# Expert loop of a hybrid network: gather with the tokens as the loaded side, and biases spread over four row groups of 32

## The chip, the core and the metric

The kernel runs on one core of one Trainium2 chip. A core has TensorE (PE, whose weight loads the profile lists apart as PEld), VectorE (DVE), ScalarE (ACT), GpSimd (POOL), SyncE (SP) and 16 DMA engines. The metric is the device time of one execution, in microseconds.

## What is computed

Two blocks run one after the other on 256 tokens of 1024 features in f32. The change lies in the last stage of the second block, a mixture of experts: 32 experts, four chosen for each token, each a clamped SwiGLU layer with two biases. The core of the reference:

```python
xb = h[tok_b]                                  # tokens of expert e
u = xb @ w1[e] + b1[e]                         # 1024 -> 2048
glu = jnp.minimum(u[:, 0::2], SWIGLU_LIMIT)
lin = jnp.clip(u[:, 1::2], -SWIGLU_LIMIT, SWIGLU_LIMIT)
act = glu * jax.nn.sigmoid(SWIGLU_ALPHA * glu) * (lin + 1.0)
return act @ w2[e] + b2[e]                     # 1024 -> 1024
...
out = out.at[slot_tok].add(slot_gate * y)      # weighted sum over the experts
```

## The kernel before

Everything is written by hand for each engine: one instruction stream per engine, ordered as the code stands, with semaphores between them. The first 1,660 us are the hybrid layers and the mixer, which the change leaves alone. Then `moe_tensor`, `moe_scalar`, `moe_vector`, `moe_pool` and `moe_loads` (SP) run the experts.

**Ahead of the loop.** The router's gates (`gate_map`, tokens x experts) are turned to `gT` (experts x tokens) by L2529 and a ScalarE copy; h is turned to `h_tok` (tokens on partitions, L2513 and the copy L2673). `start_sums` (L2539) opens the output sums in banks 0 to 3 with b2 times gT, 32 rows each. L2549 gathers for the first turn.

**The loop** runs once per job: 32 experts and as many more as there are experts with over 64 tokens; here 33 turns. One job takes at most 64 tokens (`SLOTS`). A turn `t` on PE, in order:

- L2592, the first bias: `bsel` (one-hot of the expert, 32 rows x 64 columns) is loaded and b1 (32 rows) streams, 512 columns at a time, into banks 4 and 5, halves 0 and 1 (`side`) on 64 output partitions each.
- L2601, the first product: `hsel` (gathered rows, turned) is loaded, four weight units of 2 MiB stream from the ring. After each unit e_unit is raised, and SP may overwrite the slot.
- L2549, `gather()` for turn t+1: `sel` (tokens x 64 slots, from VectorE) is loaded, `h_tok` streams, into bank 6 on 2 x 64 partitions.
- L2563, `scatter()`: the output of turn t-1 (`ye`) times `selgT` is added to banks 0 to 3.
- L2614 turns `selg` (the gates) into bank 7, ScalarE copies it to `selgT` (L2708).
- L2555, `turn_gathered()`: ScalarE has copied bank 6 to `gsel` (L2685); four transposes put it back into bank 6 turned, ScalarE copies that to `hsel` (L2688), which the next L2601 loads.
- L2621 turns `hid` (VectorE's activation) into bank 7 once `selgT` is copied; ScalarE copies it to `hidT` (L2712).
- L2629, the second product: two weight units. Then ScalarE copies to `ye` (L2715).

**The transfers.** SP issues the six units of turn t+1 one by one as the slots come free (L2438 for the first four, L2440 for the last two), after waiting for `e_unit`. There are six slots; at turn 16 the last two units come from `extra`, which is loaded ahead. b1 and b2 are loaded by L2450 after `grids`; PE and VectorE wait for all three (`late_in`).

Of the kernel before, what the change touches and what calls it, by code (L numbers as in the profile page):

```python
# [2324 lines left out]
EXTRA = 16  # L2325
JOBS = N_EXPERTS + EXTRA
# [19 lines left out]
def moe_grids():  # L2346

    o, e = np.meshgrid(np.arange(EXTRA), np.arange(N_EXPERTS), indexing="ij")
    grids = np.broadcast_to(np.concatenate([o.reshape(-1), e.reshape(-1)]), (P, 2 * GRID))
    return np.concatenate([grids, np.arange(P)[:, None]], axis=1).astype(np.float32)  # L2350


def moe_signals(ctx, nc, g, hyb):
# [22 lines left out]
def moe_memory(ctx, nc, g):  # L2376
# [8 lines left out]
    sb("b2", [D], parts=N_EXPERTS)  # L2385
    sb("b1", [2 * D_FF], parts=N_EXPERTS)
# [19 lines left out]
    sb("gT", [T], parts=N_EXPERTS)  # L2406
# [3 lines left out]
    sb("selgT", [T])  # L2410
    sb("gsel", [4 * P])
# [6 lines left out]
    sb("ye", [4 * P])  # L2418
# [13 lines left out]
def moe_loads(sp, nc, g):  # L2432
# [16 lines left out]
    for dst, what in (("grids", g["grids_dram"]), ("b2", g["b2_dram"][0]), ("b1", g["b1_dram"][0])):  # L2449
        sp.dma_start(g[dst][:, :], what).then_inc(g["late_in"].sem, g["late_in"].one())  # L2450
# [36 lines left out]
MOE_LOOP = ("e_unit", "u_first", "ga_done", "st_done", "gb_done", "ht_done")  # L2487


def moe_tensor(pe, nc, g):  # L2490
# [41 lines left out]
    def start_sums(first):  # L2532

        if first == 0:
            pe.wait_ge(g["turned_out"].sem, g["turned_out"].at(None, 2))
            pe.wait_ge(g["gates_out"].sem, g["gates_out"].at(None, 1))
            pe.wait_ge(g["late_in"].sem, g["late_in"].at(None, 3))
# [30 lines left out]
    pe.wait_ge(g["sel_ready"].sem, g["sel_ready"].at(None, 0))  # L2568
    gather().then_inc(g["ga_done"].sem, 1)
# [8 lines left out]
    def job(t, kept=0):  # L2578
# [37 lines left out]
        pe.wait_ge(g["ga_out"].sem, g["ga_out"].at(t, 1))  # L2616
        turn_gathered().then_inc(g["gb_done"].sem, g["gb_done"].one())
# [41 lines left out]
def moe_scalar(act, nc, g):  # L2659
# [408 lines left out]
```

## Time and profile before

| | us |
|---|---|
| median of 3 runs | 2665.75 |
| lowest, highest | 2664.05, 2666.48 |
| the profiled execution | 2661.23 |
| its span, first to last instruction | 2658.4 |
| PE busy | 2544.8 |
| VectorE busy | 924.9 |
| ScalarE busy | 583.4 |

The profiled execution is 4.5 us shorter than the median, and 2.8 us of it lie outside the span. All stretches below are in microseconds from the start of the span. A plain f32 matmul of the program is two load records and two matmul records in the trace, a transpose is one of each.

### The profile page before, as it was taken

How to read it: one execution, taken by the hardware profiler on the slowest of the kernel's cores; microseconds unless marked ns; L12 is line 12 of the kernel's file. 1: busy time of each engine (PE TensorE's matmuls, PEld its weight loads, DVE VectorE, ACT ScalarE, POOL GpSimd, SP SyncE). 2: the span in 40 equal slices, each digit the busy share in tenths (PEclk: the TensorE clock that was granted, in tenths of full speed). 3: DMA queues.
4: the chain of work that ended last, by engine and by line, in shares of the span. 5: the costliest groups of instructions: out<-in, count | busy, mean ns of one | idle time of the engine just before them, and what ended most of it. 6: DMA issues, size and time to landing. Idle time of an engine off the chain costs nothing.

```text
span 2658.4 us, 42182 instructions
## 1 busy us (share of the span) xinstructions
PE 2544.8 (96%) x18014; PEld 1673.4 (63%) x18014; DVE 924.9 (35%) x2004; ACT 583.4 (22%) x1168; POOL 149.5 (6%) x124
## 2 busy tenths in 40 slices
PE   8999999999999999999997889899999999999998
PEld 6867878888884887888886777433333333333333
DVE  1863363312277245323476653311111111111112
ACT  2100233301100123220135433311111111111112
POOL 0050000000032000000003220000000000000000
PEclk9999999999999999999999999999999999999999
DMA  7555232344455422336410002999999999999995
GB/s 262 198 182 198 100 122 98 124 158 159 175 204 176 173 95 96 127 128 214 162 64 4 4 4 108 420 428 428 428 428 429 428 428 427 429 428 428 429 427 251
DMA packets 135029, 636.13 MB, mean 239 GB/s; under 512 B 5120, under 2 KB 5392, under 8 KB 109136
## 3 DMA queue, kind: packets, MB, share of 16 engines
q1 hardware_dynamic: 133904, 629.78, 59.6%
q0 software_dynamic: 992, 4.37, 0.5%
q8 instruction: 109, 1.79, 0.3%
q14 instruction: 24, 0.20, 0.0%
HBM read 633.08 MB, written 1.05 MB: 239 GB/s over the span
## 4 chain that ended last, share of the span: by engine, by line
PE 94%; ACT 2%; DVE 2%; issue 1%; DMA 1%; SPq 0%; ACTq 0%; DVEq 0%
PE bank L268 26%; PE bank L2601 17%; PE bank L2629 9%; PE bank L459 6%; PE bank L1405 4%; PE bank L481 4%; PE bank L289 4%; PE bank L1356 4%; PE bank L2563 2%; PE bank L2592 2%; PE bank L2549 2%; PE bank L1664 1%; PE bank L357 1%; PE bank L2621 1%; ACT hidT L2712 1%
## 5 line engine op out<-in xcount | busy, mean ns | idle before, releaser
L268 PE MATMUL bank<-hT,ring 128*128 128x256 f32 x3136 | 689.8, 380 | 2.5 <-DMA ring<-in_w_in 1.4
L268 PEld LDWEIGHTS bank<-hT,ring 128*128 128x128 f32 x3136 | 592.8, 190 | 94.6 <-issue 13.3
L2601 PE MATMUL bank<-ring,hsel 128*64 128x512 f32 x2112 | 462.0, 595 | 0.0
L2601 PEld LDWEIGHTS bank<-ring,hsel 128*64 128x64 f32 x2112 | 149.0, 137 | 310.8 <-issue 310.5
L2874 DVE TENSOR_SCALAR glu<-bank 128x256 f32<-128x256 f32 x66 | 28.0, 425 | 754.2 <-PE bank L2601 750.9
L2629 PE MATMUL bank<-ring,hidT 128*64 128x512 f32 x1024 | 226.8, 595 | 22.0 <-ACT hidT L2712 22.0
L754 DVE SCALAR_TENSOR_TENSOR a_buf<-v_pad,par,a_buf 128x256 f32<-128x256 f32 x480 | 215.8, 529 | 0.0
L2629 PEld LDWEIGHTS bank<-ring,hidT 128*64 128x64 f32 x1024 | 70.5, 137 | 156.2 <-issue 128.1
L1405 PE MATMUL bank<-ring 64*64 64x64 f32 (+1 forms) x5696 | 133.3, 229 | 25.6 <-issue 9.3
L1405 PEld LDWEIGHTS bank<-ring 64*64 64x64 f32 x5696 | 120.9, 137 | 40.6 <-issue 12.1
L2703 ACT ACTIVATE sig<-glu 128x256 f32<-128x256 f32 x66 | 27.5, 417 | 458.8 <-DVE glu L2874 458.8
L289 PE MATMUL bank<-ring,hT 128*128 128x512 f32 x256 | 111.4, 594 | 0.0
L481 PE MATMUL bank<-ro,ring 128*128 128x256 f32 x512 | 111.4, 379 | 0.0
L481 PEld LDWEIGHTS bank<-ro,ring 128*128 128x128 f32 x512 | 97.0, 190 | 13.8 <-issue 0.8
L1356 PE MATMUL bank<-stack,ring 128*128 128x256 f32 x480 | 104.5, 379 | 0.0
L1356 PEld LDWEIGHTS bank<-stack,ring 128*128 128x128 f32 x480 | 91.1, 190 | 12.7 <-issue 0.3
L289 PEld LDWEIGHTS bank<-ring,hT 128*128 128x128 f32 x256 | 48.2, 190 | 60.0 <-issue 60.0
L1232 POOL TENSOR_TENSOR ring<-ring,mcons 128x256 f32<-128x256 f32 x80 | 62.4, 815 | 250.9 <-DVE ring L2173 250.9
L2715 ACT ACTIVATE ye<-bank 128x512 f32<-128x512 f32 x33 | 19.7, 597 | 237.2 <-PE bank L2629 237.2
L2563 PEld LDWEIGHTS bank<-selgT,ye 64*128 64x128 f32 x544 | 49.7, 186 | 33.0 <-issue 26.8
L2563 PE MATMUL bank<-selgT,ye 64*128 64x256 f32 x544 | 67.9, 389 | 0.8 <-ACT finrow L2717 0.8
L2549 PE MATMUL bank<-h_tok,sel 128*64 128x512 f32 x272 | 64.2, 592 | 0.5 <-DVE sel L2796 0.5
(435 smaller groups left out, 2467.6 us busy)
## 6 DMA issues: line engine op xcount, KB each, us to landing
ring<-in_w SPq DMA_DIRECT2D x196, 2048.0 KB, 16.7
ring<-in_w_in SPq DMA_DIRECT2D x66, 2048.0 KB, 7.8
ring<-in_w_ada SPq DMA_DIRECT2D x12, 2048.0 KB, 8.0
ring<-in_w_ret_out SPq DMA_DIRECT2D x8, 2048.0 KB, 7.8
ring<-in_w_out SPq DMA_DIRECT2D x6, 2048.0 KB, 8.6
ring<-in_w_conv_out SPq DMA_DIRECT2D x4, 2048.0 KB, 8.3
ring<-in_w_attn_out SPq DMA_DIRECT2D x4, 2048.0 KB, 8.0
extra<-in_w SPq DMA_DIRECT2D x2, 2048.0 KB, 34.7
```

The source lines that it names most:

```text
L268: mm = nc.tensor.matmul(out[:, j, :], w[:, k, col + j * P:col + (j + 1) * P], rhs[:, k, :], start=(k == 0), stop=(k == DC - 1))
L289: mm = nc.tensor.matmul(out[:, :, :].rearrange("p a b -> p (a b)"), g["hT"][:, k, t * P:(t + 1) * P], w[:, k, :], start=(k == 0), stop=(k ...
L459: mm = nc.tensor.matmul(out[:, j, :], ws[k // DC][:, k % DC, cols + j * P:cols + (j + 1) * P], rhs[:, k, :], start=(k == 0), stop=(k == n ...
L481: mm = nc.tensor.matmul(out[:, j, :], w[:, k, col:col + P], g["ro"][:, row * DC + k, :], start=(row == 0 and j == 0 and k == 0), stop=(row ...
L754: ins = nc.vector.scalar_tensor_tensor(out=y[:, c, :], in0=v[:, c, t:t + T], scalar=w, in1=y[:, c, :], op0=ALU.mult, op1=ALU.add)
L1232: nc.gpsimd.tensor_tensor(g["cut"][:, k, d * NC:(d + 1) * NC, :], g["MP"][:, d * NC:(d + 1) * NC, :], row(mask[:, k, d, :], NC), ALU.mult) ...
L1356: mm = nc.tensor.matmul(flat[(q + 3) % 4][:, 0:T], w[:, k, j * P:(j + 1) * P], g["stack"][:, k, lo:lo + T], start=(k == 0), stop=(k == DC ...
L1405: mm = nc.tensor.matmul(out[at:at + 64], lhsT[lo:lo + 64], rhs[lo:lo + 64], start=start, stop=stop, skip_group_check=not (start and stop))
L2549: mm = nc.tensor.matmul(half(flat[6], side), g["sel"][:, t, :], g["h_tok"][:, t, side * UNIT:(side + 1) * UNIT], start=(t == 0), stop=(t = ...
L2563: mm = nc.tensor.matmul(g["bank"][b][:, at, :], half(g["ye"], side)[:, n * P:(n + 1) * P], half(g["selgT"], side), start=False, stop=last, ...
L2601: mm = nc.tensor.matmul(half(flat[4 + b], side), g["hsel"][:, 2 * (j % 2) + k, j // 2, :], w[:, at:at + UNIT], start=False, stop=(j == 3 a ...
L2629: mm = nc.tensor.matmul(half(flat[7], side), g["hidT"][:, c, j, :], w[:, at:at + UNIT], start=(j == 0 and c == 0), stop=(j == 1 and c == 3))
```

## The change

- `gather()` swaps the sides: `h_tok` is the loaded side (128 columns with a step of 4, so that the order of the features is the one `hsel` needs), `sel` with its 64 columns streams. The result in bank 6 is already turned. It takes 16 matmuls of 64 columns instead of 4 of 512.
- `turn_gathered()`, `gsel`, `take_gathered()` and the semaphores `ga_out` and `gb_done` are gone. ScalarE copies bank 6 to `hsel` right after the gather.
- b1 and b2 are cut in four parts and loaded to four groups of 32 partitions, by eight DMAs instead of two. `bsel` and `gT` are repeated on the four groups. The four matmuls of the first bias use one group each; `start_sums` is called once and goes round the four groups, one bank each.
- The gate map is turned by eight plain matmuls into four groups of 32 output partitions instead of two transposes.
- The first gather waits for `h_tok`'s second half.

```diff
+GROUPS = P // N_EXPERTS
...
-    for dst, what in (("grids", g["grids_dram"]), ("b2", g["b2_dram"][0]), ("b1", g["b1_dram"][0])):
-        sp.dma_start(g[dst][:, :], what).then_inc(g["late_in"].sem, g["late_in"].one())
+    sp.dma_start(g["grids"][:, :], g["grids_dram"]).then_inc(g["late_in"].sem, g["late_in"].one())
+    for name, width in (("b2", D // GROUPS), ("b1", 2 * D_FF // GROUPS)):
+        for q in range(GROUPS):
+            sp.dma_start(g[name][q * N_EXPERTS:(q + 1) * N_EXPERTS, :],
+                         g[name + "_dram"][0, :, q * width:(q + 1) * width]).then_inc(g["late_in"].sem, g["late_in"].one())
...
     for t in range(TC):
-        mm = nc.tensor.transpose(flat[7][0:N_EXPERTS, t * P:(t + 1) * P], g["gate_map"][:, t, 0:N_EXPERTS], ident)
+        for q in range(GROUPS):
+            mm = nc.tensor.matmul(flat[7][q * N_EXPERTS:(q + 1) * N_EXPERTS, t * P:(t + 1) * P], g["gate_map"][:, t, 0:N_EXPERTS],
+                                  ident, start=True, stop=True)
...
-        for n in range(first, first + 4):
-            nc.tensor.matmul(g["bank"][n // 2][:, n % 2, :], g["b2"][:, n * P:(n + 1) * P], g["gT"][:, :],
-                             start=(n % 2 == 0), stop=False, skip_group_check=True)
+        for i in range(2):
+            for q in range(GROUPS):
+                lo, hi = q * N_EXPERTS, (q + 1) * N_EXPERTS
+                nc.tensor.matmul(g["bank"][q][:, i, :], g["b2"][lo:hi, i * P:(i + 1) * P], g["gT"][lo:hi, :],
+                                 start=(i == 0), stop=False, skip_group_check=True)
...
     def gather():
 
-        for t in range(TC):
-            for side in range(2):
-                mm = nc.tensor.matmul(half(flat[6], side), g["sel"][:, t, :], g["h_tok"][:, t, side * UNIT:(side + 1) * UNIT],
-                                      start=(t == 0), stop=(t == 1))
-        return mm
-
-    def turn_gathered():
         for c in range(4):
-            mm = nc.tensor.transpose(flat[6][:, c * P:(c + 1) * P], g["gsel"][:, c::4], ident)
+            for j in range(2):
+                for t in range(TC):
+                    mm = nc.tensor.matmul(flat[6][:, (2 * c + j) * SLOTS:(2 * c + j + 1) * SLOTS],
+                                          g["h_tok"][:, t, j * UNIT:(j + 1) * UNIT][:, c::4], g["sel"][:, t, :],
+                                          start=(t == 0), stop=(t == 1))
         return mm
...
     pe.wait_ge(g["sel_ready"].sem, g["sel_ready"].at(None, 0))
+    pe.wait_ge(g["turned_out"].sem, g["turned_out"].at(None, 2))
     gather().then_inc(g["ga_done"].sem, 1)
-    start_sums(0)
-    pe.wait_ge(g["ga_out"].sem, g["ga_out"].at(None, 0))
-    turn_gathered().then_inc(g["gb_done"].sem, 1)
-    start_sums(4)
+    start_sums()
...
         for b in range(2):
             for side in range(2):
-                at = (2 * side + b) * UNIT
-                nc.tensor.matmul(half(flat[4 + b], side), g["bsel"][0:N_EXPERTS, :], g["b1"][:, at:at + UNIT], start=True, stop=False)
+                lo, hi = (2 * side + b) * N_EXPERTS, (2 * side + b + 1) * N_EXPERTS
+                nc.tensor.matmul(half(flat[4 + b], side), g["bsel"][lo:hi, :], g["b1"][lo:hi, :], start=True, stop=False)
...
-        pe.wait_ge(g["ga_out"].sem, g["ga_out"].at(t, 1))
-        turn_gathered().then_inc(g["gb_done"].sem, g["gb_done"].one())
...
         act.wait_ge(g["ga_done"].sem, g["ga_done"].at(t, 1))
-        take_gathered().then_inc(g["ga_out"].sem, g["ga_out"].one())
+        take_rows().then_inc(g["gt_out"].sem, g["gt_out"].one())
         act.wait_ge(g["st_done"].sem, g["st_done"].at(t, 1))
         nc.scalar.activation(g["selgT"][:, :], flat[7][:, 0:T], ACT.Copy).then_inc(g["st_out"].sem, g["st_out"].one())
-        act.wait_ge(g["gb_done"].sem, g["gb_done"].at(t, 1))
-        take_rows().then_inc(g["gt_out"].sem, g["gt_out"].one())
```

PE in a turn of the loop, from the end of the first product to the second product. A row names output, streamed side and loaded side, and the count; h_tok is the tokens, sel the choice. Before:

```order
L2601 MATMUL bank<-ring,hsel 64x512 x8
L2549 MATMUL bank<-h_tok,sel 64x512 x4
L2563 MATMUL bank<-selgT,ye 128x256 x8
L2614 MATMUL bank<-shared_cons,selg 128x128 x2
L2555 MATMUL bank<-shared_cons,gsel 128x128 x4
L2621 MATMUL bank<-shared_cons,hid 128x128 x4
L2629 MATMUL bank<-ring,hidT 64x512 x16
```

And now:

```order
L2602 MATMUL bank<-ring,hsel 64x512 x8
L2556 MATMUL bank<-sel,h_tok 128x64 x16
L2566 MATMUL bank<-selgT,ye 128x256 x8
L2615 MATMUL bank<-shared_cons,selg 128x128 x2
L2620 MATMUL bank<-shared_cons,hid 128x128 x4
L2628 MATMUL bank<-ring,hidT 64x512 x16
```

The gather has 16 instructions of 64 streamed columns in the place of 4 of 512, and no transposes stand between those of selg and those of hid.

PE ahead of the loop, from the gates to the first product (b is b2 in L2539 and b1 in L2592). Before:

```order
L2529 MATMUL bank<-shared_cons,gate_map 32x128 x2
L2549 MATMUL bank<-h_tok,sel 64x512 x4
L2539 MATMUL bank<-gT,b 128x256 x4
L2555 MATMUL bank<-shared_cons,gsel 128x128 x4
L2539 MATMUL bank<-gT,b 128x256 x4
L2592 MATMUL bank<-b,bsel 64x512 x4
```

And now:

```order
L2533 MATMUL bank<-shared_cons,gate_map 32x128 x8
L2556 MATMUL bank<-sel,h_tok 128x64 x16
L2545 MATMUL bank<-gT,b 128x256 x8
L2593 MATMUL bank<-b,bsel 64x512 x4
```

The opening of the sums is in one piece; its count and that of the first bias are unchanged, only their rows differ.

## Rows read from the trace of the kernel before

**Rows 1.** The page: engine busy times, and the chain by engine.
```profile
PE 2544.8 (96%) x18014; PEld 1673.4 (63%) x18014; DVE 924.9 (35%) x2004; ACT 583.4 (22%) x1168; POOL 149.5 (6%) x124
...
PE 94%; ACT 2%; DVE 2%; issue 1%; DMA 1%; SPq 0%; ACTq 0%; DVEq 0%
```

**Rows 2.** The chain in order of time, one turn: start us, us, what.
```profile
2580.53 1.86 PE bank L2592 x8
2582.39 13.88 PE bank L2601 x64
2596.27 1.72 PE bank L2549 x8
...
2600.29 0.48 PE bank L2555 x4
...
2609.29 1.86 PE bank L2592 x8
```

**Rows 3.** Windows: stretch, its length, busy us of each engine, granted clock, DMA share, GB/s.
```profile
1675.50:1682.00 6.50, 4.39 (x33) 3.19 (x34) 5.35 (x32) 3.44 (x9) 0.00 (x0) 1.00 1.03 436
1689.10:1692.30 3.20, 3.20 (x10) 1.01 (x10) 2.76 (x5) 1.51 (x2) 0.00 (x0) 0.50 1.03 440
...
1718.00:2580.00 862.00, 841.40 (x4140) 315.03 (x4136) 118.97 (x360) 146.56 (x240) 0.00 (x0) 1.00 1.01 428
```

**Rows 4.** Unit transfers: first of the loop; fourth unit of the last turn; PE reaching it.
```profile
DMA to landing us min/median/max: 9.8/9.8/9.8
...
L2438 SPq DMA_DIRECT2D ring<-in_w x1: 333/333/333, 2596.5 to 2596.5; - x1
...
DMA to landing us min/median/max: 24.3/24.3/24.3
...
2621.00 0.14 PEld L2601 LDWEIGHTS bank<-ring,hsel 128*64 128x64 f32 x2 [0.29 <-DMA ring<-in_w]
```

**Rows 5.** Timeline of the weight loads: start us, us, line, out<-streamed,loaded, shapes, count.
```profile
31.83 1.08 PEld L242 LDWEIGHTS bank<-cons,weighed 128*128 128x128 f32 x8
...
1678.53 0.30 PEld L2521 LDWEIGHTS bank<-chosen_map,moec 128*128 128x128 f32 x2 [1.61 <-DVE chosen_map L2767]
...
1679.20 0.53 PEld L2525 LDWEIGHTS bank<-chosen_map,shared_cons 128*128 128x128 f32 x4
```

**Rows 6.** The page's groups: count, busy us, mean ns.
```profile
L268 PE MATMUL bank<-hT,ring 128*128 128x256 f32 x3136 | 689.8, 380 | 2.5 <-DMA ring<-in_w_in 1.4
...
L2549 PE MATMUL bank<-h_tok,sel 128*64 128x512 f32 x272 | 64.2, 592 | 0.5 <-DVE sel L2796 0.5
```

**Rows 7.** Groups of 1718 to 2580, and the timeline of the selgT copy and L2621.
```profile
L2621 PEld LDWEIGHTS bank<-shared_cons,hid 128*128 128x128 f32 x120 | 16.8, 209 | 5.5 <-ACT selgT L2708 5.5
...
2600.32 0.39 ACT L2708 ACTIVATE selgT<-bank 128x256 f32<-128x256 f32 x1 [1.69 <-PE bank L2614]
...
2600.76 0.56 PEld L2621 LDWEIGHTS bank<-shared_cons,hid 128*128 128x128 f32 x4 [0.18 <-ACT selgT L2708]
```

**Rows 8.** Timeline and groups where tiles of the array run together.
```profile
14.84 1.92 PE L232 MATMUL bank<-ring,cond 128*32 128x512 f32 x16
...
L1405 PE MATMUL bank<-ring 64*64 64x64 f32 (+1 forms) x192 | 3.7, 230 | 0.6 <-ACT ring L1833 0.6
```

**Rows 9.** Timeline ahead of the loop, up to the first product.
```profile
1676.32 2.06 ACT L2673 ACTIVATE h_tok<-bank 128x512 f32<-128x512 f32 x4 [0.23 <-PE bank L2513]
...
1680.97 1.94 PE L2549 MATMUL bank<-h_tok,sel 128*64 128x512 f32 x8 [0.51 <-DVE sel L2796]
...
1682.06 0.68 DVE L2829 TENSOR_TENSOR before<-ends,grids 128x512 f32<-128x512 f32 x1
...
1689.36 15.46 PE L2601 MATMUL bank<-ring,hsel 128*64 128x512 f32 x64
```

**Rows 10.** SP's issues ahead of the loop, and the longest landing of a bias.
```profile
1658.36 0.81 SPq L2438 DMA_DIRECT2D ring<-in_w  x2
...
b<-in_b_dram SPq DMA_DIRECT2D x1, 256.0 KB, 13.8
```

More of the change, by code:

```diff
@@ L2349, in moe_grids @@
     grids = np.broadcast_to(np.concatenate([o.reshape(-1), e.reshape(-1)]), (P, 2 * GRID))
-    return np.concatenate([grids, np.arange(P)[:, None]], axis=1).astype(np.float32)
+    return np.concatenate([grids, np.arange(P)[:, None] % N_EXPERTS], axis=1).astype(np.float32)
 def moe_signals(ctx, nc, g, hyb):
@@ L2359, in moe_signals @@
     for name, spent, base, per in (
-        ("u_first", "x_sum", 0, 1), ("ga_done", "conv_sum", 1, 1), ("gb_done", "ret_scores", 1, 1), ("st_done", "ret_o", 1, 1),
-        ("ht_done", "ret_var", 0, 1), ("ga_out", "x_root", 1, 1), ("st_out", "conv_root", 1, 1), ("ht_out", "decay_ready", 0, 1),
+        ("u_first", "x_sum", 0, 1), ("ga_done", "conv_sum", 1, 1), ("st_done", "ret_o", 1, 1),
+        ("ht_done", "ret_var", 0, 1), ("st_out", "conv_root", 1, 1), ("ht_out", "decay_ready", 0, 1),
         ("bsel_ready", "x_squared", 1, 1), ("selg_ready", "h_ready", 0, 1), ("hid_ready", "decay_sum", 0, 1),
@@ L2384, in moe_memory @@
     g["ec"] = lambda name: g["moec"][:, MOE_CONST[name][0]:MOE_CONST[name][1]]
-    sb("b2", [D], parts=N_EXPERTS)
-    sb("b1", [2 * D_FF], parts=N_EXPERTS)
+    sb("selgT", [T])
+    sb("ye", [4 * P])
+    sb("b2", [D // GROUPS])
+    sb("b1", [2 * D_FF // GROUPS])
     sb("grids", [2 * GRID + 1])
@@ L2405, in moe_memory @@
     sb("jobs", [JOBS], mybir.dt.int32)
-    sb("gT", [T], parts=N_EXPERTS)
+    sb("gT", [T])
     sb("sel", [TC, SLOTS])
@@ L2409, in moe_memory @@
     sb("bsel", [SLOTS])
-    sb("selgT", [T])
-    sb("gsel", [4 * P])
     sb("hsel", [4, 2, SLOTS])
@@ L2484, in moe_pool @@
     nc.gpsimd.memset(g["selgT"][:, :], 0.0).then_inc(g["zeros_set"].sem, g["zeros_set"].one())
-MOE_LOOP = ("e_unit", "u_first", "ga_done", "st_done", "gb_done", "ht_done")
+MOE_LOOP = ("e_unit", "u_first", "ga_done", "st_done", "ht_done")
 def moe_tensor(pe, nc, g):
@@ L2528, in moe_tensor, with start_sums @@
     for t in range(TC):
-        mm = nc.tensor.transpose(flat[7][0:N_EXPERTS, t * P:(t + 1) * P], g["gate_map"][:, t, 0:N_EXPERTS], ident)
+        for q in range(GROUPS):
+            mm = nc.tensor.matmul(flat[7][q * N_EXPERTS:(q + 1) * N_EXPERTS, t * P:(t + 1) * P], g["gate_map"][:, t, 0:N_EXPERTS],
+                                  ident, start=True, stop=True)
     mm.then_inc(g["gates_turned"].sem, g["gates_turned"].one())
[L2532 to L2537, printed above, removed]
-        for n in range(first, first + 4):
-            nc.tensor.matmul(g["bank"][n // 2][:, n % 2, :], g["b2"][:, n * P:(n + 1) * P], g["gT"][:, :],
-                             start=(n % 2 == 0), stop=False, skip_group_check=True)
+    def start_sums():
+        pe.wait_ge(g["turned_out"].sem, g["turned_out"].at(None, 2))
+        pe.wait_ge(g["gates_out"].sem, g["gates_out"].at(None, 1))
+        pe.wait_ge(g["late_in"].sem, g["late_in"].at(None, 1 + 2 * GROUPS))
+        for i in range(2):
[3 more added lines that the diff above has]
+                                 start=(i == 0), stop=False, skip_group_check=True)
     def half(bank, side):
@@ L2680, in moe_scalar @@
     act.wait_ge(g["gates_turned"].sem, g["gates_turned"].at(None, 1))
-    nc.scalar.activation(g["gT"][:, :], flat[7][0:N_EXPERTS, 0:T], ACT.Copy).then_inc(
+    nc.scalar.activation(g["gT"][:, :], flat[7][:, 0:T], ACT.Copy).then_inc(
         g["gates_out"].sem, g["gates_out"].one())
-    def take_gathered():
-        return nc.scalar.activation(g["gsel"][:, :], flat[6], ACT.Copy)
     def take_rows():
@@ L2810, in moe_vector @@
     tally, over, ends = g["tally"], g["over"], g["ends"]
-    v.tensor_copy(g["bhot"][:, 0:N_EXPERTS], g["c"]("ident")[:, 0:N_EXPERTS])
+    v.tensor_copy(g["bhot"][:, 0:N_EXPERTS], g["ec"]("fold"))
     v.tensor_scalar(over[:, :], tally[:, :], float(SLOTS), None, ALU.is_gt).then_inc(g["e_dve"].sem, g["e_dve"].one())
@@ L2823, in moe_vector @@
         g["turns_set"].sem, g["turns_set"].one())
-    dve.wait_ge(g["late_in"].sem, g["late_in"].at(None, 3))
+    dve.wait_ge(g["late_in"].sem, g["late_in"].at(None, 1 + 2 * GROUPS))
     grid_o = g["grids"][:, 0:GRID].rearrange("p (o e) -> p o e", o=EXTRA)
@@ L2962, in program @@
         moe["moe_in"] = Signal(ctx, nc, "moe_in", 3, 16)
-        moe["late_in"] = Signal(ctx, nc, "late_in", 3, 16)
+        moe["late_in"] = Signal(ctx, nc, "late_in", 1 + 2 * GROUPS, 16)
         moe["e_dve"] = follow(mix["init_dve"], INIT_DVE, None)
```

4 lines of the change are left out of this document (1 added, 3 removed).

## The prediction

> **What bounds the kernel now.** I read the engine table first [rows 1]: TensorE (PE) is busy 96% of the span, VectorE 35%, ScalarE 22%. The chain that ended last is 94% PE. Of the expert loop the window from 1,718 to 2,580 us shows PE busy 841.4 of 862 us and the DMA engines' share at 1.01, 428 GB/s [rows 3]. So the loop has two candidates for a bound, and the question is which one waits.
>
> The chain over one turn of the loop [rows 2] has no wait for a transfer. The pieces that matter here are L2592 1.86 us (first bias), L2601 13.88 (first product), L2549 1.72 (gather) and L2555 0.48 (turn of the gathered rows). From one L2592 to the next it is 2609.29 - 2580.53 = 28.76 us. The DMA side is slower: a turn brings six transfers of 2 MiB, 12.58 MB, at 428 GB/s 29.4 us [rows 3]. PE outruns it by 0.6 us a turn and lives off its lead: from issue to landing a unit takes 9.8 us at the start of the loop and 24.3 us for the fourth unit of the last turn, which is issued at 2596.5 and lands at 2620.8, and PE reaches it at 2621.0 with an idle ended by that landing [rows 4]. The lead is used up exactly at the end. **Two consequences:** a shorter turn on PE gives next to nothing, since the transfers then end the loop at today's time; a longer one is paid 33 times over, from the first 0.1 us on, since PE then ends the loop and no transfer does.
>
> **Gather, part by part.** Before, sel is the loaded side (64 columns) and 512 columns stream: 4 matmuls, 8 records, two at a time, 1.72 us on the chain. Now h_tok is loaded (128x128, with a step of 4 elements) and 64 columns stream: 16 matmuls. A plain f32 matmul leaves two records each with its own load, as L2525 does (2 instructions, x4), so there are 32 loads of 128x128 in a row. The nearest rows are the rank sums: from L2521 at 1678.53 to L2525 at 1679.20 six loads start (two each of L2521, L2522 and L2523), 0.112 us a load, while each streams only 32 columns [rows 5]. L242 streams 2 columns and still takes 1.08 us for 8 loads, (1.08 - 0.19) / 7 = 0.127: less streaming doesn't speed it up, so the load is the pace. Streaming itself is 256 columns in 689.8 / 3136 = 0.22 us [rows 6], so 64 columns are 0.055 and hide behind the next load. The step of 4 may cost a little: L2555 loads with that step, four in 0.48 us on the chain, 0.120 [rows 2]. I take 0.12: 32 x 0.12 = 3.84. The array's shape also changes once more on each side of the gather; L2592 shows what that costs: 1.86 for four pairs of records, where L2549, which keeps the shape of L2601, takes 1.72 for four, so 0.14. About 4.0 us instead of 1.72: **+2.25 us a turn**, from +1.95 (0.112 a load, 0.1 for the change) to +2.5 (0.123, and 0.3 around it).
>
> **Turn of the gathered rows.** L2555's four transposes and ScalarE's gsel copy go. The chain shows 0.48 us for them, but the next step, L2621, isn't waiting for them: its loads wait for ScalarE's selgT copy, 5.5 us in 30 turns, 0.18 each; the copy runs from 2600.32 to 2600.71, L2621 starts at 2600.76 [rows 7]. That copy starts when L2614 is done and stands in the way with or without L2555. I take **0** for PE. ScalarE has slack [rows 1]; the hsel copy now follows the gather and is needed only at the next L2601, about 12 us later.
>
> **First bias.** Four matmuls of 32 rows and 512 columns, 8 records. All use rows 0 to 31 now, so only the two column halves run together: 1.86 us. Now each has its own 32 rows. L232 has four column groups and runs 16 records of 512 columns in 1.92 us, four at a time. L1405 (64x64 in two row and two column groups) runs 192 in 3.7 us; at 0.055 each that is 2.8 at a time, which two column groups alone can't give, so row groups run together, and its two row groups write one bank [rows 8]. Two steps of 0.43 (a quarter of 1.72) and 0.14: 1.0 us, **-0.86 us a turn**; bounds 0 (groups of 32 rows don't overlap; no row has them) and -0.86.
>
> The Trainium skill, "TensorEngine Tiling (Array Packing)", Gotcha 1, says that different row tiles cannot access the same PSUM bank at once. Here both sides of one b write one bank from different row groups; by that rule the saving is lost, the first rival below holds, and the time is 2738. L1405's 2.8 at a time speaks against it for different partitions of a bank.
>
> **Sum of the loop.** 2.25 - 0.86 = +1.39 us a turn, to 30.15, above the 29.4 us of the transfers, so PE is the bound throughout. All 33 turns (L2549's 272 records are 34 gathers of 8, one of them ahead of the loop [rows 6]) pay it, the last too, whose gather nobody reads: 33 x 1.39 = **+45.9 us**.
>
> **Ahead of the loop.** From L2549 at 1680.97 to L2601 at 1689.36 are 8.39 us [rows 9]. New: gather 4.1, second bias 1.0 (16 records of 256 columns four at a time, instead of one by one at 0.22, 3.5 us and two changes of shape), L2555 gone, first bias 1.15: 6.25, **-2.1 us**. The clock is granted at 0.50 from 1689.1 to 1692.3 (1.2 instead of 2.4 GHz), right after a stretch in which PE ran L2539 and L2592, matmuls of 32 rows [rows 3]; the first L2601 takes 15.46 us [rows 9], later ones 13.9. With half of those matmuls' time left I expect that stretch to go: **-1.5 us**, bounds -1.5 and +1.7 (it falls on the gather).
>
> Edits that cost nothing: six more DMA issues on SP, 0.5 us each, put the fourth to sixth unit and the two extras 3 us later, but the two units issued from 1658.4 on keep the engines busy for 9.8 us [rows 10], and by the sum above unit 3 is read only at about 1,697 (1687.2 and three units of 3.45). The biases land 13.8 us after issue, 1,674 to 1,677, and the first reader behind that wait is VectorE at 1682.1 [rows 9, 10]. The gate map is now turned by 16 records in four column groups instead of 2, in a 0.5 us gap in which PE waits for sel. The added wait for h_tok ahead of the first gather is over at 1678.4, when ScalarE has written it [rows 9]. If that cover failed, each is under 3 us, once.
>
> **Total:** 45.9 - 2.1 - 1.5 = +42.3 us. The profiled execution took 2661.23 us with a span of 2658.4, the median is 2665.75. On the profiled one 2703.5, on the median **2708 us**, 1.6% slower. Bounds of this case: 33 x (1.95 - 0.86) - 3.6 = +32, 2698; 33 x (2.5 - 0.86) - 0.4 = +54, 2720.
>
> **Rivals.**
> *The bias saves nothing* (groups of 32 rows run no better than one group does today). 33 x 2.25 - 2 = +72, 2738. For it: no row shows groups of 32 rows together. Against: L1405.
>
> *The gather is as cheap as today, and the result is not slower.* If the 32 loads overlap each other or the loads shrink with the 64 streamed columns, the gather takes no more than about 2.7 us (0.08 a record) and a turn stays below 28.9 us. Then PE saves at most its wait and the transfers decide: the fourth unit of the last turn lands at 2620.8 whatever PE does, and behind it stands today's path. That gives 2665 to 2668. Against it: the loads in a row at 0.112 [rows 5]. For faster than that the transfers would have to end earlier, and their share is 1.01 from 1,718 to 2,580 [rows 3].
>
> *The gather is dearer.* Loads don't overlap with streaming, so 0.112 + 0.055 = 0.167 a record: 1.5 us more a turn, 33 x 2.9 - 2 = +94, 2760; about the same if the light gather brings the half clock in every turn. Against: L268 streams 256 columns every 0.22 us with its loads hidden, and the clock stays 1.00 from 1675.5 to 1682.0, where PE is as lightly used [rows 3, 6].
>
> The Trainium skill, "TensorE: Matmul & The Clock Gate", "The mechanism" in Part 3, states that loads overlap with running matmuls only when the row group differs; by that rule this rival would hold, 2760. L268 uses one and the same row group and overlaps, so the trace disagrees.
>
> **How the numbers follow.** Forecast 0.76; bias saves nothing 0.06; not slower 0.11; dearer 0.07. The range takes the forecast's bounds and reaches to the first rival, 2696 to 2740, which leaves 0.18 out. A measurement here can tell about 0.2%, 5.3 us. Faster by more 0.03, within 0.08 (the rest of the second rival), slower 0.89.
>
> **What the profile will show.** A turn, from one first bias to the next, of 30.15 us (29.9 to 30.4), and no wait of PE for a transfer; such waits, with turns of 29.4 us, would mean the second rival. 32 loads of 128x128 in the gather about 0.12 apart, 4.0 us; 0.17 is the third rival. The bias in 1.0 us; 1.86 is the first. The transposes of hid still start right behind the selgT copy. DMA at about 417 GB/s in the loop, issue to landing no longer growing to 24 us but shrinking. I am wrong if loads of 128x128 behind one another with a step of 4 go faster than their rows here.

## The result: 247 us slower, not 42

The changed kernel takes 2912.45 us, median of 4 runs (2907.06 to 2917.76), the kernel before 2664.9 us (4 runs on the same chip). The ratio is 1.0932, 95% interval 1.0906 to 1.0958: slower by about 247 us. The prediction said 2708 with a range from 2696 to 2740. The profiled run took 2907.06 us with a span of 2904.8, where the kernel before had 2658.4; the difference of these two spans, 246.4 us, is what is accounted for below.

The page of the changed kernel: busy times, granted clock and the groups of the gather (in a group: count | busy us, mean ns of one | idle before):

```profile
PE 2777.9 (96%) x18708; PEld 1922.4 (66%) x18708; DVE 926.9 (32%) x2004; ACT 563.7 (19%) x1134; POOL 149.7 (5%) x124
...
PEclk9999999999999999999999979989898898988888
...
L268 PEld LDWEIGHTS bank<-hT,ring 128*128 128x128 f32 x3136 | 592.8, 190 | 94.4 <-issue 13.3
...
L2556 PEld LDWEIGHTS bank<-sel,h_tok 128*128 128x128 f32 x1088 | 256.4, 328 | 27.3 <-issue 26.8
...
L2566 PE MATMUL bank<-selgT,ye 64*128 64x256 f32 x544 | 120.8, 617 | 0.8 <-ACT finrow L2709 0.8
```

Beside [rows 1] the share looks alike: TensorE (PE) is 96% busy in both. Three things differ. PE has 233 us more to do. A load of the gather lasts 328 ns on average, where the 128x128 loads of L268 last 190. And the granted clock is no longer 9 in every slice of the loop but 8 and 9 in turn; the scatter behind the gather, L2566, shows it with 617 ns a record on average, against 389 in the kernel before.

The chain of waits over one turn of the loop, and the piece of the next one where it differs (start us, us, what):

```profile
2558.55 1.02 PE bank L2593 x8
2559.57 13.88 PE bank L2602 x64
2573.46 7.66 PE bank L2556 x32
2581.12 3.46 PE bank L2566 x16
2584.57 0.38 PE bank L2615 x2
...
2585.41 0.76 PE bank L2620 x4
...
2586.85 7.09 PE bank L2628 x32
2593.94 1.02 PE bank L2593 x8
...
2608.84 7.66 PE bank L2556 x32
2616.49 3.72 PE bank L2566 x16
...
2621.30 1.14 PE bank L2620 x4
...
2623.12 9.76 PE bank L2628 x32
```

Against [rows 2]: the first bias (L2593, was L2592) takes 1.02 us instead of 1.86, the gather (L2556, was L2549) 7.66 instead of 1.72. This turn lasts 2593.94 - 2558.55 = 35.39 us. The scatter L2566 behind the gather takes 3.46 us, and in the next turn the transposes of hid (L2620) and the second product (L2628) are slow too, 1.14 and 9.76 instead of 0.76 and 7.09.

The windows of the changed kernel (stretch, its length, busy us by engine, clock, DMA share, GB/s) say why: first the start of the gather, then its second half with the scatter, the same and on into the second product one turn later, and the stretch of [rows 3]:

```profile
2573.46:2576.60 3.14, 3.14 (x14) 3.14 (x14) 2.28 (x6) 0.48 (x2) 0.00 (x0) 1.00 0.99 423
2577.60:2584.40 6.80, 6.80 (x32) 5.87 (x31) 0.42 (x2) 0.60 (x1) 0.00 (x0) 0.52 1.02 434
2612.00:2628.00 16.00, 14.84 (x54) 9.34 (x55) 1.02 (x4) 1.58 (x3) 0.00 (x0) 0.50 0.61 260
...
1718.00:2580.00 862.00, 835.06 (x3767) 425.69 (x3767) 96.40 (x284) 101.67 (x166) 0.00 (x0) 0.88 0.82 342
```

In every turn the clock falls to 0.50 (1.2 instead of 2.4 GHz) within the gather, 2.7 to 5.8 us after its start, and comes back 7 to 17 us after it fell. The DMA engines, at a share of 1.01 before, now have 0.82: no transfer is waited for.

The whole loop, from the first to the last record of the first bias, in the changed kernel and in the one before (min, median and max ns, then first and last start in us):

```profile
L2593 PE MATMUL bank<-b,bsel x264: 587/638/1110, 1688.1 to 2849.9; 32*64 32x512 f32 x132
```
```profile
L2592 PE MATMUL bank<-b,bsel x264: 587/587/734, 1687.4 to 2610.6; 32*64 32x512 f32 x132
```

That is 1161.8 against 923.2 us, and 0.8 more between the starts of the groups, since the last group itself is shorter now: 32 turns cost 239.4 us more, 7.5 each. The gather is 5.94 of it and the bias -0.84. About 2.4 us a turn remain, and the clock is the candidate: added up over the run, the scatter is 53 us longer (120.8 us busy against 67.9 of L2563), the second product 19 (245.7 against 226.8) and the transposes of selg and hid together 6. Two questions for the experiments: why a load takes twice what [rows 5] showed, and whether the clock really owns the rest.

The loads of one gather, as one row of the timeline (start us, us, count), give the pace, (7.54 - 0.31) / 31 = 0.233 us from load to load, where 0.31 is one load by itself:

```profile
2573.38 7.54 PEld L2556 LDWEIGHTS bank<-sel,h_tok 128*128 128x128 f32 x32 [0.81 <-issue]
```

### The profile page after: what moved, and what is told of

Same layout as the page of the kernel before. It is cut to its first block, busy times and chain, and to the rows that moved or that the text cites. A ratio compares the mean times of both kernels' runs of the same rounds, so it can differ in the third digit from the quotient of the medians.

```text
span 2904.8 us, 43543 instructions
## 1 busy us (share of the span) xinstructions
PE 2777.9 (96%) x18708; PEld 1922.4 (66%) x18708; DVE 926.9 (32%) x2004; ACT 563.7 (19%) x1134; POOL 149.7 (5%) x124
## 4 chain that ended last, share of the span: by engine, by line
PE 94%; ACT 3%; DVE 2%; issue 1%; DMA 0%; SPq 0%; ACTq 0%; DVEq 0%
PE bank L268 23%; PE bank L2602 16%; PE bank L2556 9%; PE bank L2628 9%; PE bank L459 6%; PE bank L2566 4%; PE bank L1405 4%; PE bank L481 4%; PE bank L289 4%; PE bank L1356 4%; PE bank L2593 1%; PE bank L1664 1%; PE bank L2620 1%; PE bank L357 1%; ACT hidT L2704 1%
## 5 line engine op out<-in xcount | busy, mean ns | idle before, releaser
L268 PE MATMUL bank<-hT,ring 128*128 128x256 f32 x3136 | 689.7, 380 | 2.4 <-DVE hT L719 2.4
L268 PEld LDWEIGHTS bank<-hT,ring 128*128 128x128 f32 x3136 | 592.8, 190 | 94.4 <-issue 13.3
L2556 PEld LDWEIGHTS bank<-sel,h_tok 128*128 128x128 f32 x1088 | 256.4, 328 | 27.3 <-issue 26.8
L2628 PE MATMUL bank<-ring,hidT 128*64 128x512 f32 x1024 | 245.7, 636 | 22.0 <-ACT hidT L2704 22.0
L2556 PE MATMUL bank<-sel,h_tok 128*128 128x64 f32 x1088 | 262.8, 419 | 0.3 <-DVE sel L2788 0.3
L2628 PEld LDWEIGHTS bank<-ring,hidT 128*64 128x64 f32 x1024 | 75.0, 146 | 172.1 <-issue 142.5
L1405 PEld LDWEIGHTS bank<-ring 64*64 64x64 f32 x5696 | 120.5, 137 | 38.9 <-issue 11.5
L2566 PE MATMUL bank<-selgT,ye 64*128 64x256 f32 x544 | 120.8, 617 | 0.8 <-ACT finrow L2709 0.8
L2566 PEld LDWEIGHTS bank<-selgT,ye 64*128 64x128 f32 x544 | 83.5, 316 | 22.4 <-ACT finrow L2709 1.7
```

Source lines behind the costliest of these rows:

```text
L268: mm = nc.tensor.matmul(out[:, j, :], w[:, k, col + j * P:col + (j + 1) * P], rhs[:, k, :], start=(k == 0), stop=(k == DC - 1))
L1405: mm = nc.tensor.matmul(out[at:at + 64], lhsT[lo:lo + 64], rhs[lo:lo + 64], start=start, stop=stop, skip_group_check=not (start and stop))
L2556: mm = nc.tensor.matmul(flat[6][:, (2 * c + j) * SLOTS:(2 * c + j + 1) * SLOTS], g["h_tok"][:, t, j * UNIT:(j + 1) * UNIT][:, c::4], g["se ...
L2566: mm = nc.tensor.matmul(g["bank"][b][:, at, :], half(g["ye"], side)[:, n * P:(n + 1) * P], half(g["selgT"], side), start=False, stop=last, ...
L2628: mm = nc.tensor.matmul(half(flat[7], side), g["hidT"][:, c, j, :], w[:, at:at + UNIT], start=(j == 0 and c == 0), stop=(j == 1 and c == 3))
```

## Experiments

**1. The same gather from neighbouring elements.** Theory: the step of 4 in the loaded side is what a load pays for.

```diff
-            ins = nc.scalar.activation(g["h_tok"][:, t, b * UNIT:(b + 1) * UNIT], flat[2 * t + b], ACT.Copy)
+            ins = nc.scalar.activation(g["h_tok"][:, t, b * UNIT:(b + 1) * UNIT].rearrange("p (c i) -> p c i", c=4),
+                                       flat[2 * t + b].rearrange("p (i c) -> p c i", c=4), ACT.Copy)
...
-                                          g["h_tok"][:, t, j * UNIT:(j + 1) * UNIT][:, c::4], g["sel"][:, t, :],
+                                          g["h_tok"][:, t, j * UNIT + c * P:j * UNIT + (c + 1) * P], g["sel"][:, t, :],
```

> The changed kernel with one thing different: ScalarE writes h_tok with the features of each half in the order c, c+4, c+8, ... (its copy out of PSUM is reordered), so that the gather's 32 loads of 128x128 read neighbouring elements and not every fourth. Same matmuls, same counts, same result. Theory A (the step of 4 elements in the loaded side makes a load take 0.233 us): loads start 0.112 us apart as in the rank sums before the loop, the gather takes 3.6 to 4.0 us instead of 7.7, the granted clock stays at 1.00 through the loop, a turn takes about 30 us and the kernel 2695 to 2710. Theory B (0.233 us is what any f32 load of 128x128 takes that has only 64 streamed columns behind it, or what loads take while six transfers a turn write SBUF): the gather stays at 7.5 us or more, the clock falls as before, and the time stays at 2905 to 2920. Mixed case: loads at 0.112, but the gather still lets the clock fall to 0.50 behind it; then the turn is 31.5 to 32.5 us and the time 2750 to 2780.

Measured: 2702.09 us (2698.94 to 2704.82), 1.0133 of the kernel before (1.0113 to 1.0152). Chain, timeline of the loads and window, all of this kernel:

```profile
2440.02 1.02 PE bank L2593 x8
...
2454.92 3.71 PE bank L2556 x32
2458.64 1.93 PE bank L2566 x16
...
2469.93 0.57 PE bank L2593
```
```profile
2454.85 3.65 PEld L2556 LDWEIGHTS bank<-sel,h_tok 128*128 128x128 f32 x32 [0.81 <-issue]
```
```profile
1718.00:2580.00 862.00, 829.50 (x4564) 369.22 (x4560) 116.91 (x346) 123.44 (x201) 0.00 (x0) 1.00 0.99 415
```

Loads are (3.65 - 0.19) / 31 = 0.112 us apart, where 0.19 is one load by itself; the gather takes 3.71 us, the clock stays at 1.00, a turn takes 29.91 us. Nothing but the distance of the elements was changed in the loop, and 210 us are gone, the dearer loads and the half clock behind them together. Theory A holds, theory B falls. PE is still the bound and the DMA share 0.99.

**2 and 3. Each half of the change alone.** Bias alone is the changed kernel with the old gather and its transposes; gather alone is the kernel before with the new gather. The edits are the two halves of the diff ahead.

> The kernel before with the other half of the change alone: both biases in four row groups of 32, gather and transposes as before. Theory A (transfers set the end of the kernel before, as the prediction said): a turn of PE's own work is 0.85 us shorter, but PE then waits for unit transfers near the end of the loop, and the time stays within 2655 to 2668. Rival (PE's own work is the bound): the whole 33 x 0.85 = 28 us and some 2 ahead of the loop appear, 2633 to 2640. If the row groups do not run together, a first bias stays at 1.86 us and the time at 2665.

> The kernel before with the gather of the change alone (h_tok loaded with a step of 4, no transposes behind it), both biases as before. Theory A: the whole loss is the gather's, its own 5.9 us a turn and the half clock of 2.1 us; the time is the changed kernel's plus 33 x 0.85, 2930 to 2950, loads 0.233 us apart. Rival (the half clock comes from the bias with 32 rows or from both together): the clock stays at 1.00 in the loop, and the time is about 2880.

Measured: bias alone 2661.95 us, ratio 0.9984 (0.9974 to 0.9994); gather alone 2960.27 us, ratio 1.1106 (1.1085 to 1.1128). The chain of the bias-only kernel over one turn, and its share by engine on the page:

```profile
2596.52 0.04 issue
...
2600.40 25.52 DMA ring<-in_w
2625.91 0.04 issue
```
```profile
PE 73%; DMA 22%; ACT 2%; DVE 2%; issue 1%; SPq 0%; ACTq 0%; DVEq 0%
```

Some 28 us of PE's work are gone, and the time falls by 2.8. The chain goes through the transfers now, 2625.91 - 2596.52 = 29.39 us a turn, which is the 29.4 that the prediction had worked out from [rows 3]. The turns in which PE has no such wait last 27.91 us instead of 28.76. So the bias does take 0.84 us less, and it pays next to nothing while the transfers set the end.

The gather-only kernel, the opening of its sums ahead of the loop (start us, us) and its window:

```profile
1687.18 7.19 PE L2538 MATMUL bank<-gT,b 32*128 32x256 f32 x16
```
```profile
1718.00:2580.00 862.00, 835.29 (x3625) 419.84 (x3625) 91.71 (x273) 98.59 (x161) 0.00 (x0) 0.88 0.79 329
```

The gather alone is slower by 48 us than the whole change (2960.27 against 2912.45), and the spans of the two profiled executions differ by 2958.5 - 2904.8 = 53.7. Of that, 33 x 0.84 = 28 are the bias. The rest was not expected. 5.1 us are the opening of the sums, which belongs to the other half of the change: here its matmuls run one after another, and at the half clock, 7.19 us against 2.09. Most of what remains is what the half clock hits in the loop. Its turns repeat 36.2, 36.7 and 39.7 us, and the slow second product comes every third turn, where the changed kernel has it every fifth, so the second product is 10 us longer over the run. The window shows a mean clock of 0.88, as in the changed kernel: the clock is not lower, it falls in other places of the turn. So the rival of run 3, that the small bias matmuls bring the half clock, falls too: with the old bias the clock falls all the same.

**4. The pace of a load against the step.** Four steps in one kernel, eight loads each (other features are gathered than the reference wants).

```diff
-                                          g["h_tok"][:, t, j * UNIT:(j + 1) * UNIT][:, c::4], g["sel"][:, t, :],
+                                          g["h_tok"][:, t, :][:, 0:P * (1, 2, 3, 8)[c]:(1, 2, 3, 8)[c]], g["sel"][:, t, :],
```

> The changed kernel, in which the gather's loaded side has step 1 for c = 0, step 2 for c = 1, step 3 for c = 2 and step 8 for c = 3, eight loads each, taken from h_tok's first features (so other features than the reference's are gathered; the amount of work is the same). Read off the time from load to load for each c. Theory A with a cost by 16-byte lines (a load pays for each line that it touches beyond one for two elements): 0.112 us at steps 1 and 2, 0.17 to 0.233 at step 3, 0.233 at step 8, the same as at 4. Theory A with a cost by distance: 0.112, 0.15, 0.19 and over 0.4 us. Theory B: 0.233 at all four.

The timeline of the loads of one gather, steps 1, 2, 3 and 8:

```profile
2539.65 0.97 PEld L2556 LDWEIGHTS bank<-sel,h_tok 128*128 128x128 f32 x8 [0.81 <-issue]
...
2540.54 1.02 PEld L2556 LDWEIGHTS bank<-sel,h_tok 128*128 128x128 f32 x8
...
2541.48 1.47 PEld L2556 LDWEIGHTS bank<-sel,h_tok 128*128 128x128 f32 x8
...
2542.87 1.99 PEld L2556 LDWEIGHTS bank<-sel,h_tok 128*128 128x128 f32 x8
```

With one load's own duration in the trace, 0.19, 0.20, 0.26 and 0.33 us, taken off and the rest divided by 7: 0.111, 0.117, 0.173 and 0.237 us. The clock was granted at 1.00 for all but the last 0.4 us of them. Together with 0.233 at step 4 this is no cost by distance, since 8 costs what 4 costs, but one by 16-byte pieces: 128 elements touch 32, 64, 96, 128 and 128 of them, and 1.82 ns each (0.233 / 128) gives 0.058, 0.117, 0.175, 0.233 and 0.233. The pace is the larger of this and the 0.112 of a contiguous load. A step of 2 is almost free, 3 costs half as much again, 4 and 8 twice as much. The kernel took 2817.85 us in its one run, with the clock at 0.93 from 1718 to 2580 us: its gather of 5.3 us still brings the half clock in most turns.

The Trainium skill, "SBUF — State Buffer", in the note on SBUF "cachelines" under "Door 1", says that SBUF has lines of 16 bytes, that two hits a line are needed for full bandwidth and that each access which crosses to a new line pays. These rows agree with that. The same note says that one can therefore stride 4 fp32 for free; here step 3 already costs 0.06 us a load and step 4 0.12, so the rows disagree with the figure.

**5. The clock's share.** The changed kernel, its loads untouched, with four times the streaming (its output is no longer the reference's).

```diff
-                    mm = nc.tensor.matmul(flat[6][:, (2 * c + j) * SLOTS:(2 * c + j + 1) * SLOTS],
-                                          g["h_tok"][:, t, j * UNIT:(j + 1) * UNIT][:, c::4], g["sel"][:, t, :],
+                    mm = nc.tensor.matmul(flat[6][:, (c // 2) * 4 * SLOTS:(c // 2 + 1) * 4 * SLOTS],
+                                          g["h_tok"][:, t, j * UNIT:(j + 1) * UNIT][:, c::4], row(g["sel"][:, t, :], 4),
                                           start=(t == 0), stop=(t == 1))
```

> The changed kernel with its step of 4, in which each of the gather's matmuls streams sel's 64 columns four times over (256 columns instead of 64; it writes a region of the gather's bank four times as wide, so each region keeps the features of the last c that wrote it and the output is not the reference's). Loads stay as they are. A record's streaming of 256 columns takes 0.21 to 0.22 us at the full clock, just under the 0.233 from load to load. Theory A (the half clock behind the gather comes from TensorE doing little in these 7.5 us): the gather stays at 7.5 to 7.8 us, the granted clock stays at 1.00 in the whole loop, a turn is 33.8 to 34.0 us (35.97 less the 2.1 put down to the clock) and the time is 2835 to 2850 us, shorter than the changed kernel although four times as much streams. Rival (the clock falls for another reason, such as the slow loads themselves or the six transfers a turn): the clock falls as before, and the time is 2905 to 2930. Second rival: loads of this kind don't overlap with a longer stream; the gather takes 14 us, and the time is above 3050.

Measured: 2836.1 us (2831.85 to 2839.09), ratio 1.0642 (1.0617 to 1.0666). Four times the columns stream in the gather, and the kernel is 76 us faster than the changed one. Chain, window, and the first and last record of the first bias:

```profile
2522.82 7.77 PE bank L2556 x32
2530.59 1.93 PE bank L2566 x16
```
```profile
1718.00:2580.00 862.00, 832.12 (x4010) 421.42 (x4012) 101.80 (x302) 109.90 (x179) 0.00 (x0) 1.00 0.88 364
```
```profile
L2593 PE MATMUL bank<-b,bsel x264: 587/610/638, 1692.7 to 2780.1; 32*64 32x512 f32 x132
```

The gather is as long as before (7.77 us), so the loads still set its pace, but the clock stays at 1.00 and the scatter is back at 1.93. The loop is 1161.8 - 1087.4 = 74.4 us shorter, and the gather itself 0.11 us a turn longer, so the half clock cost (74.4 + 32 x 0.11) / 32 = 2.4 us a turn. What brings it is that PE streams so little in a gather this long. The transfers don't, and the slow loads alone don't: both are here too. The slow loads have a part all the same, since they make the stretch of light streaming 7.7 us long: in run 1 the same 64 columns behind each load, in 3.71 us, left the clock at 1.00 in the loop. The second rival falls as well, since 256 columns stream beside each load and the loads stay 0.233 apart.

**6, 7 and 8. What exactly pays.** [Rows 7] and [rows 2] had shown transposes with a step of 4 at 0.12 us. Run 6 is run 1 with 16 transposes of steps 1, 2, 4 and 8 (L2621) ahead of the turn of hid, which it makes with plain matmuls (L2623).

```diff
+        for step in (1, 2, 4, 8):
+            for c in range(4):
+                nc.tensor.transpose(flat[7][:, c * P:(c + 1) * P], g["h_tok"][:, 0, :][:, 0:P * step:step], ident)
         for c in range(4):
-            mm = nc.tensor.transpose(flat[7][:, c * P:(c + 1) * P], g["hid"][:, c::4], ident)
+            mm = nc.tensor.matmul(flat[7][:, c * P:(c + 1) * P], g["hid"][:, c::4], ident, start=True, stop=True)
```

> The kernel of contiguous loads, in which the four transposes of hid (step of 4 in hid) are ordinary matmuls with the identity (same result), and ahead of them stand 16 transposes of h_tok's features that nobody reads, four each with steps 1, 2, 4 and 8 in the loaded side. Question: why L2555 and L2621 of the kernel before showed 0.12 us for a load with a step of 4. Theory A1 (a transpose is another kind of load, which the step does not touch): the 16 transposes start 0.11 to 0.13 us apart at every step, and the matmuls of hid take 8 loads at 0.233, 1.9 to 2.1 us instead of 0.76. Theory A2 (a short burst of four loads runs ahead of the cost): transposes slow down to 0.233 from the fifth load of steps 4 and 8 on, and the matmuls of hid start with some loads at 0.12. Theory A3 (it is the 128 streamed columns beside the load, not the operation): transposes as in A1, but the matmuls of hid also at 0.12, 1.0 us. Turn: 29.9 plus 1.9 plus 1.2, about 33 us; time about 2800.

```profile
2507.77 0.42 PEld L2621 LDWEIGHTS bank<-shared_cons,h_tok 128*128 128x128 f32 x4 [0.71 <-ACT selgT L2706]
...
2508.16 0.56 PEld L2621 LDWEIGHTS bank<-shared_cons,h_tok 128*128 128x128 f32 x4
...
2508.62 0.69 PEld L2621 LDWEIGHTS bank<-shared_cons,h_tok 128*128 128x128 f32 x5
...
2509.11 0.54 PEld L2621 LDWEIGHTS bank<-shared_cons,h_tok 128*128 128x128 f32 x4
...
2509.56 1.94 PEld L2623 LDWEIGHTS bank<-shared_cons,hid 128*128 128x128 f32 x8
```

The four rows of L2621 in the timeline are steps 1, 2, 4 and 8 (the third also holds the first load of step 8). The 16 transposes take 2.07 us on the chain, none more than 0.125 behind the one before. The plain matmuls behind them load hid with the same step and the same shape at (1.94 - 0.31) / 7 = 0.233. A2 and A3 fall: it isn't a burst that runs ahead, and it isn't the width of the stream. The operation decides; a transpose's load doesn't pay for a step, up to 8. The kernel took 2806.73 us in its one run.

Run 7 is the changed kernel with four shapes of the gather's loads, eight each (its output is not the reference's).

```diff
+            rows, wide, n = ((P, P // 2, SLOTS), (32, P, SLOTS), (P, P, 8), (P, P, SLOTS))[c]
...
+                    every = g["h_tok"][0:rows, t, 0:wide * 4:4]
+                    if c == 3:
+                        every = g["h_tok"][:, :, :].rearrange("p a b -> p (a b)")[:, 8 * t:2 * D:16]
```

> The changed kernel, in which the gather's matmuls have four shapes, eight loads each: c = 0 loads 64 columns with a step of 4; c = 1 loads 128 columns with a step of 4 from 32 rows only; c = 2 is the gather's load with 8 columns streamed instead of 64; c = 3 has a step of 16 (other features and fewer products than the reference's, so its output differs). If the cost is 1.82 ns for each 16-byte line that one partition's row touches (runs with steps 1, 2, 3, 4 and 8 gave 0.112, 0.118, 0.173, 0.233 and 0.238 us, and 32, 64, 96, 128 and 128 lines are 0.058, 0.117, 0.175, 0.233 and 0.233): 0.117 us for 64 columns, 0.233 for 32 rows, 0.233 for 8 streamed columns, 0.233 to 0.24 for step 16. Rival (the cost grows with the amount read over all partitions): 32 rows at 0.112. Rival (it grows slowly with the distance): step 16 at 0.26 or more. Rival (load and stream add up): 8 streamed columns below 0.21.

```profile
2527.25 0.91 PEld L2560 LDWEIGHTS bank<-sel,h_tok 128*64 128x64 f32 x7 [0.24 <-issue]
...
2528.23 1.94 PEld L2560 LDWEIGHTS bank<-sel,h_tok 32*128 32x128 f32 x8
...
2530.23 1.94 PEld L2560 LDWEIGHTS bank<-sel,h_tok 128*128 128x128 f32 x8
...
2532.08 1.84 PEld L2560 LDWEIGHTS bank<-sel,h_tok 128*128 128x128 f32 x8
```

The 64-column load (the first of its eight stands apart, ahead of the row) takes (0.91 - 0.19) / 6 = 0.12, the one of 32 rows and the one with 8 streamed columns (1.94 - 0.31) / 7 = 0.233. So the cost goes with the columns loaded, not with the rows, and what streams beside it doesn't matter. Step 16 takes (1.84 - 0.31) / 7 = 0.219, a little less than 8; the simple rule said 0.233, and no run explains the difference. The kernel took 2842.15 us in its one run.

Run 8 is run 1 with 16 plain matmuls that load the identity and stream features with steps 1, 2, 4 and 8.

```diff
+        for step in (1, 2, 4, 8):
+            for c in range(4):
+                nc.tensor.matmul(flat[7][:, c * P:(c + 1) * P], ident, g["h_tok"][:, 0, :][:, 0:P * step:step],
+                                 start=True, stop=True)
```

> The kernel of contiguous loads, with 16 plain matmuls that nobody reads ahead of the transposes of hid: the identity is loaded (neighbouring elements) and 128 of h_tok's features stream, four matmuls each (eight records) with steps 1, 2, 4 and 8. The transposes of the run before took 0.11 to 0.125 us at every step where a plain matmul took 0.233, with the turned tile on the side that the profile names as loaded. Question: does the step cost on the streamed side what it costs on the loaded side? Theory S1 (only the loading of a plain matmul pays by 16-byte lines; streaming 128 columns needs 0.107 us at the full clock and hides reads of its lines): records start 0.107 to 0.125 us apart at all four steps, the 32 of them take 3.6 to 4.0 us, and a turn is about 33.6 us. Theory S2 (any read by TensorE passes 1.82 ns a line): 0.107, 0.117, 0.233 and 0.233 us, 5.6 us in all, and a turn of 35.5 us. With S2 the transposes would have to be cheap for a reason of their own; with S1 it may be that a transpose streams the tile that it turns.

```profile
2529.32 1.07 PE L2621 MATMUL bank<-h_tok,shared_cons 128*128 128x128 f32 x8
...
2530.24 2.00 PE L2621 MATMUL bank<-h_tok,shared_cons 128*128 128x128 f32 x8
...
2532.05 2.05 PE L2621 MATMUL bank<-h_tok,shared_cons 128*128 128x128 f32 x8
```

The rows are steps 2, 4 and 8. One record lasts 0.28 us in the first and 0.41 in the others, so step 2 has (1.07 - 0.28) / 7 = 0.113 from record to record, step 4 (2.00 - 0.41) / 7 = 0.227 and step 8 0.234 (step 1, not shown, starts a record every 0.112). S2 holds: the streamed side pays the same price, and the 32 records take 5.77 us on the chain. Swapping the sides doesn't avoid it. Then a transpose is the exception, whichever side it reads its tile through, and why stays open. The kernel took 2883.37 us in its one run.

No version beats the kernel before by more than the bias alone does, 0.16%: the transfers hold the end at 29.4 us a turn, and the shortest turn with the new gather is 29.91.

## Why the prediction was wrong, point by point

**What bounds the kernel** was right, both ways. A longer PE turn is paid in full: the 1.15 us of run 1 appear in each of its turns (29.91 against 28.76). A shorter one is not: the bias alone.

**The gather term failed, and it is the cause of the miss.** The step reads "The step of 4 may cost a little: L2555 loads with that step, four in 0.48 us on the chain, 0.120 [rows 2]. I take 0.12: 32 x 0.12 = 3.84." It cost 0.233: 7.66 us instead of 4.0, +5.94 us a turn instead of +2.25, 33 x 3.69 = 122 us. The rows were read rightly, but they couldn't carry the number. [Rows 5] are plain loads of neighbouring elements, and L2555 and L2621 are transposes. No row of the kernel before shows a plain load with a step. The one property that was new was priced from another operation, and both bounds (0.112 and 0.123) came from rows that lack one of the two properties. The last sentence of the prediction asked only whether such loads might go faster. For contiguous loads the term was good, and a little high: 3.71 measured in run 1, 4.0 predicted. 32 x 0.112 = 3.58 leaves 0.13 for what stands around the loads, close to the 0.14 of the term, so it was the 0.12 that was high.

**The clock in the loop** stood in the third rival alone, at 0.07 together with dearer loads. It cost 2.4 us a turn, 78 us in all. The evidence against it was that the clock stays at 1.00 from 1675.5 to 1682.0 [rows 3], "where PE is as lightly used". That stretch is no longer than one gather is now, and right behind comparable work the kernel before does have its half clock (1689.1 to 1692.3 in the same rows). A stretch at full clock doesn't show that the work in it leaves the clock alone; one has to look at what follows too. The rival named the half clock rightly, but its reason for dear loads was wrong: loads and streaming don't add up, since the pace is 0.233 with 8, 64 and 256 streamed columns (run 7, the changed kernel, run 5). And 0.167 a load and 1.5 us a turn were both too small, so 2760 was still 150 us short.

**The first bias** was right: -0.84 measured, -0.86 predicted. The Trainium skill's Gotcha 1 in "TensorEngine Tiling (Array Packing)", weighed there, would have lost this saving; both sides of one b write one bank from different groups of rows in the changed kernel and take 1.02 us, so the trace disagrees in this case. The first rival, that the bias saves nothing, fell.

**Turn of the gathered rows at 0** was right: from the end of L2615 to the start of L2620 only ScalarE's selgT copy stands (2584.95 to 2585.41), as in [rows 7].

**Ahead of the loop** I had -2.1 and -1.5 us. The timeline of the changed kernel there:

```profile
1678.45 7.73 PE L2556 MATMUL bank<-sel,h_tok 128*128 128x64 f32 x32 [0.27 <-DVE sel L2788]
1686.11 2.09 PE L2545 MATMUL bank<-gT,b 32*128 32x256 f32 x16
1688.13 1.93 PE L2593 MATMUL bank<-b,bsel 32*64 32x512 f32 x8
```

And the window over it:

```profile
1679.60:1689.90 10.30, 10.30 (x52) 7.91 (x52) 9.46 (x20) 3.69 (x9) 0.00 (x0) 0.50 1.00 426
```

From the gather to the first product (1689.99) are 11.5 us instead of 8.39, and from 1679.6 on the clock is at 0.50. The half clock did leave the first product, 13.88 us instead of 15.29, close to the -1.5; it came earlier instead and took the gather and both biases. In run 5, where the clock stays full, the second and the first bias take 1.15 and 1.09 us, where 1.0 and 1.15 were predicted. The contiguous gather of run 1 falls into the half clock here too and takes 7.09 us. There the half clock costs 3.3 us in the gather (7.09 against the 3.79 of the same record in the loop) and 1.4 in the two biases (2.02 and 1.52), less 1.4 in the first product, so even with contiguous loads the upper bound would have had to be +3.3, not +1.7. Contiguous loads are 0.213 us apart there; loads with a step of 4 take 0.23 at either level of the clock.

**The sum of the changed kernel**, on the profiled runs: gather 33 x 5.94 = +196.0, bias 33 x -0.84 = -27.7, half clock in the loop +77.9, first product at the full clock -1.4, start of the first bias +0.8 (1688.1 against 1687.4), together 245.6 of the 246.4 measured.

**Would the forecast have been right with contiguous loads?** Run 1 says so: 2702.09 us, inside 2696 to 2740. But two errors cancel in it, a gather 0.25 us a turn cheaper than its term (-8 us) and a stage ahead of the loop that gains nothing: 10.6 us from gather to first product instead of 8.39, less 1.4 in that product, +0.8 where -3.6 stood (+4.4).

## What to carry to other kernels

Before swapping the sides of a matmul, look at the step of what becomes the loaded side: a plain f32 operand whose elements are 16 bytes or more apart takes about twice the time of a contiguous one, on either side, and the fix is to write the tensor in the order in which it will be read (here in a ScalarE copy ahead of the loop; it gives back 210 us). Price a new operation from a row with the same operation and the same access pattern; where there is none, the range has to stay open upward, since a transpose is no stand-in for a matmul. Where many loads stand in a row and little streams, count also what the half clock costs the work behind, and don't expect a saving on PE to show where the transfers set the end.

## What the runs showed of the hardware

- From load to load of a plain f32 load of 128 columns, by the step of its elements: 0.111 (1), 0.117 (2), 0.173 (3), 0.233 (4), 0.237 (8), 0.219 us (16). 64 columns with step 4 take 0.12, 32 rows as much as 128. At the half clock contiguous loads are 0.213 apart and those with step 4 still 0.233.
- The streamed side pays the same: 0.112, 0.113, 0.227 and 0.234 us for 128 columns at steps 1, 2, 4 and 8.
- A transpose of 128x128 takes 0.11 to 0.125 us at steps 1, 2, 4 and 8. Why isn't known.
- A gather of 7.7 us in which 64 columns stream behind each load lets the granted clock fall to 0.50, and the price is paid by the work behind it; with 256 columns behind each load, in the same time, it stays at 1.00 and the kernel is 76 us faster. With 64 columns behind each load in a gather of 3.7 us it stays at 1.00 in the loop too.
- Plain f32 matmuls of 32 rows in four groups of rows, each two of them writing different partitions of one bank, run together: 8 records in 1.02 us against 1.86.
